# A hybrid diffusion layer in fp32 split matmuls: the order of work between the two halves, and the last stores

## The reference

```python
def rmsnorm(x, g=None):
    xf = x.astype(jnp.float32)
    y = xf * lax.rsqrt(jnp.mean(xf * xf, axis=-1, keepdims=True) + EPS)
    if g is not None:
        y = y * g.astype(jnp.float32)
    return y.astype(x.dtype)

def layer(x, cond, l, mixer):
    mod = (jax.nn.silu(cond) @ w_mod[l] + b_mod[l])[:, None, :]
    sh_m, sc_m, g_m, sh_f, sc_f, g_f = jnp.split(mod, 6, axis=-1)
    h = rmsnorm(x, norm_g[l, 0]) * (1.0 + sc_m) + sh_m
    m, ctx_out = mixer(h @ w_in[l], l)
    x = x + g_m * rmsnorm(m @ w_out[l], norm_g[l, 1])
    h = rmsnorm(x, norm_g[l, 2]) * (1.0 + sc_f) + sh_f
    a, g = jnp.split(h @ w_ffn_in[l], 2, axis=-1)
    x = x + g_f * rmsnorm((jax.nn.silu(g) * a) @ w_ffn_out[l], norm_g[l, 3])
    return x, ctx_out
```

## Time and profile before

| what | us |
|---|---|
| median of 3 timed runs (1798.84 to 1799.16) | 1798.86 |
| the profiled execution's own time | 1798.27 |
| its span, first to last instruction | 1796.4 |
| TensorE busy | 1763.2 (98%) |
| VectorE busy | 947.0 (53%) |
| ScalarE busy | 659.8 (37%) |
| GpSimd busy | 125.9 (7%) |
| FFN matmuls that take 384 columns (L1158), three passes of 1408 each | 471.4, 470.4, 470.3 |

### The profile page before, as it was taken

The page is one execution under the profiler, slowest core; times in us unless marked ns, Lnnn a source line. Parts: engine busy times, 40 slices in busy tenths (PEclk is TensorE's granted clock), DMA queues, the critical chain, the costliest instruction groups (busy, mean ns, idle before and its releaser), DMA issues.

```text
span 1796.4 us, 22651 instructions
## 1 busy us (share of the span) xinstructions
PE 1763.2 (98%) x9499; PEld 1526.4 (85%) x9499; DVE 947.0 (53%) x1276; ACT 659.8 (37%) x952; POOL 125.9 (7%) x172
## 2 busy tenths in 40 slices
PE   5999999999999999999999999999999999999998
PEld 4667666677778879999999999999999988888886
DVE  5554578633657677356656633333333455555554
ACT  3422354443464344222222222222222344454542
POOL 1001045420300010000000000000000000000000
PEclk9999999999999999999999999999999999999999
DMA  9988777775322242345454443433333333333331
GB/s 395 349 331 318 299 270 273 294 265 228 114 104 94 104 177 117 118 172 203 167 207 188 182 147 117 140 118 124 135 117 140 119 124 134 117 138 121 121 113 71
DMA packets 47046, 317.37 MB, mean 177 GB/s; under 512 B 5433, under 2 KB 7665, under 8 KB 10017
## 3 DMA queue, kind: packets, MB, share of 16 engines
q1 hardware_dynamic: 44592, 305.35, 45.4%
q0 software_dynamic: 2288, 10.56, 1.8%
q10 hardware_dynamic: 64, 0.02, 0.0%
HBM read 310.52 MB, written 5.39 MB: 176 GB/s over the span
## 4 chain that ended last, share of the span: by engine, by line
PE 93%; DVE 3%; DMA 2%; ACT 1%; issue 0%; POOL 0%; SPq 0%; DVEq 0%; POOLq 0%; ACTq 0%
PE ps L1158 41%; PE ps L934 7%; PE ps L936 7%; PE ps L935 7%; PE ps L828 7%; PE ps L829 7%; PE ps L827 7%; PE ps L806 3%; DMA raw<-in_weights 2%; PE ps L1048 1%; PE ps L1071 1%; DVE wlo L1224 1%; PE ps L1106 1%; PE ps L894 1%; PE ps L896 1%; PE ps L895 1%
## 5 line engine op out<-in xcount | busy, mean ns | idle before, releaser
L1224 DVE TENSOR_TENSOR wlo<-raw,whi 128x1024 fp32r<-128x1024 f32 x376 | 459.8, 1236 | 692.6 <-ACT whi L460 692.1
L460 ACT ACTIVATE whi<-raw 128x1024 fp32r<-128x1024 f32 x376 | 392.3, 1058 | 829.7 <-PE ps L1158 507.0
L1158 PE MATMUL ps<-h_hi,whi 128*128 128x384 f32 x1408 | 471.4, 335 | 0.5 <-DVE h_lo L1303 0.5
L1158 PE MATMUL ps<-h_hi,wlo 128*128 128x384 f32 x1408 | 470.4, 334 | 0.0
L1158 PE MATMUL ps<-h_lo,whi 128*128 128x384 f32 x1408 | 470.3, 334 | 0.0
L1158 PEld LDWEIGHTS ps<-h_hi,whi 128*128 128x128 f32 x1408 | 264.3, 188 | 0.7 <-issue 0.7
L1158 PEld LDWEIGHTS ps<-h_lo,whi 128*128 128x128 f32 x1408 | 264.3, 188 | 0.0
L1158 PEld LDWEIGHTS ps<-h_hi,wlo 128*128 128x128 f32 x1408 | 264.3, 188 | 0.0
L934 PE MATMUL ps<-whi,h_hi 128*128 128x512 f32 x624 | 259.8, 416 | 0.2 <-DVE wlo L1224 0.2
L936 PE MATMUL ps<-wlo,h_hi 128*128 128x512 f32 x624 | 244.5, 392 | 0.0
L935 PE MATMUL ps<-whi,h_lo 128*128 128x512 f32 x624 | 243.6, 390 | 0.0
(11 more groups left out here) (257 smaller groups left out, 1363.6 us busy)
## 6 DMA issues: line engine op xcount, KB each, us to landing
raw<-in_weights SPq DMA_DIRECT2D x278, 1024.0 KB, 4.9
raw_x<-in_weights SPq DMA_DIRECT2D x6, 1024.0 KB, 18.5
xT<-in_x_t SPq DMA_DIRECT2D x4, 768.0 KB, 7.0
out<-x_sb SPq DMA_DIRECT2D x6, 512.0 KB, 2.7
x_sb<-in_x_sample POOLq DMA_DIRECT2D x1, 2048.0 KB, 11.0
sbc<-silu_rows POOLq DMA_DIRECT2D x1, 2048.0 KB, 8.2
gw<-in_lru_gate_w SPq DMA_DIRECT2D x4, 256.0 KB, 3.3
out<-U POOLq DMA_DIRECT2D x4, 256.0 KB, 5.6
```

Source lines behind the costliest of these rows:

```text
L460: nc.scalar.activation(whi[:, 2 * (g % RING) + b], raw_of(t)[:, HK * b:HK * b + HK].rearrange("p k n -> p (k n)"), ACT.Copy).then_inc(w_hi, 1)
L1158: return nc.tensor.matmul(ps[bank][:, 0:T], w[:, k % KH * P:(k % KH + 1) * P], xs[:, k, :], start=first, stop=last)
L1224: V.tensor_tensor(wlo[:, 2 * SLOT[t] + b], raw_of(t)[:, HK * b:HK * b + HK].rearrange("p k n -> p (k n)"), whi[:, 2 * (g % RING) + b].bitc ...
```

## The change

Four edits. VectorE runs `residual(2)` ahead of `norm_diagonal(0)`. Block 2's squares are taken in four instructions of 512 columns (`x1_parts`), each behind its own L1609, and POOL adds four sums. In the first FFN tile pair TensorE waits for h_hi, runs the four matmuls of one k that read h_hi, then waits for h_lo and runs the two that read it. The last block is added and stored in three pieces of 1024, 512 and 512 columns (`y_parts`). The numbers of the fillers stay 26, 10 and 5.

```diff
-    xss, xrs, xsh = small("xss", 3), small("xrs", 3), small("xsh", 6)
+    xss, xrs, xsh = small("xss", 3), small("xrs", 3), small("xsh", 8)
...
+        def y_parts(tb):
+            ends = [0, D // 2, D] if tb < TB - 1 else [0, D // 2, D - NC, D]
+            return [slice(a, b) for a, b in zip(ends, ends[1:])]
+
+        def x1_parts(tb):
+            return 4 if tb == TB - 1 else 2
...
-                for b in range(2):
-                    part = slice(D // 2 * b, D // 2 * (b + 1))
+                for b, part in enumerate(y_parts(tb)):
                     sp.wait_ge(fin, 2 * tb + b + 1)
                     sp.dma_start(y_p[0, :, part] if tb == 0 else y_s[0, (tb - 1) * P:tb * P, part], x_sb[:, tb, part]).then_inc(out_st, 16)
-            sp.wait_ge(out_st, 2 * TB * 16)
+            sp.wait_ge(out_st, (2 * TB + 1) * 16)
...
-                for b in range(2):
+                w = D // x1_parts(tb)
+                for b in range(x1_parts(tb)):
                     act.wait_ge(x1_ok, 2 * tb + b + 1)
-                    nc.scalar.activation(dump[:, 2 * tb + b, :], x_sb[:, tb, D // 2 * b:D // 2 * (b + 1)], ACT.Square,
+                    nc.scalar.activation(dump[:, 2 * tb + b * w // (D // 2), b * w % (D // 2):b * w % (D // 2) + w],
+                                         x_sb[:, tb, w * b:w * (b + 1)], ACT.Square,
                                          scale=D ** -0.5, accum_out=xsh[:, 2 * tb + b:2 * tb + b + 1]).then_inc(sq_done, 1)
...
-                pe.wait_ge(x1_ok, 2 * tb + 2)
+                pe.wait_ge(x1_ok, 2 * tb + x1_parts(tb))
...
+                pe.wait_ge(h_hs, KD + k + 1)
+                for part in range(2):
+                    b, wh, wl = now[part]
+                    up(k, part, wh, h_hi, k == 0, False)
+                    up(k, part, wl, h_hi, False, False)
                 pe.wait_ge(h_ls, KD + k + 1)
                 for part in range(2):
                     b, wh, wl = now[part]
-                    ins = up_k(k, part, wh, wl)
+                    ins = up(k, part, wh, h_lo, False, k == KD - 1)
...
-                    if n % 2:
+                    if n % 2 or tb == TB - 1:
                         ins.then_inc(x1_ok, 1)
...
             residual(1)
+            residual(2)
             norm_diagonal(0)
-            residual(2)
...
-                for b in range(2):
-                    c = slice(D // 2 * b, D // 2 * (b + 1))
+                for c in y_parts(tb):
                     V.scalar_tensor_tensor(x_sb[:, tb, c], y2[:, tb, c], yrs[:, tb:tb + 1], x_sb[:, tb, c],
                                            ALU.mult, ALU.add).then_inc(fin, 1)
...
-                pool.wait_ge(sq_done, 4 + 2 * tb + 2)
-                link(G.tensor_tensor(r, r, xsh[:, 2 * tb + 1:2 * tb + 2], ALU.add))
+                for b in range(1, x1_parts(tb)):
+                    pool.wait_ge(sq_done, 4 + 2 * tb + b + 1)
+                    link(G.tensor_tensor(r, r, xsh[:, 2 * tb + b:2 * tb + b + 1], ALU.add))
```

## The result

The changed kernel takes 1802.01 us in the median of 19 runs (1800.61 to 1804.36), the kernel before 1799.16 us in 19 runs (1797.94 to 1801.35). The ratio is 1.0017 with a 95% interval of 1.001 to 1.0023: slower by about 3 us. The forecast was 1799.7 (1797.4 to 1801.5), so the direction was right and the size was not. The profiled execution has a span of 1799.8 us (1796.4 before) and took 1801.61.

A forecast was written before the change was run, and what follows sets the result against it. TensorE's pace was taken to bound the kernel behind 682 us. Terms +1.5 - 0.65 + 0 = +0.85, taken as +0.9 with the tail's +0.05, gave 1799.7 us; range 1797.4 to 1801.5, the forecast's own 1798.9 to 1800.5.

The forecast's parts named there:

- Part 1 on VectorE: Between the halves: residual 2 done 0.98 us sooner, diagonal 0 started 2.59 us later, at 675.07.
- Part 1 on TensorE, fillers in an in-order queue: Between the halves: fillers behind block 0's transposes come onto the path, block 2's transposes start 1.5 us later.
- the seams: Two passages on TensorE without a wait, allowed for in the +1.5; at 0.15 us, a released wait's cost, +1.75.
- Rival (a): Between the halves: fillers are no obstacle, diagonal 2 sets the FFN's start; -1.1 us, 1797.8; chance 0.12.
- The clock: TensorE's idle stretch before block 0's transposes: 3.75 us, where it was 1.15; the sum adds no clock loss.
- rival (c): TensorE's idle stretch before block 0 drops the clock: 0 to +6.9 us, +3.5 at half, 1803.2; chance 0.10.
- Part 2, squares in quarters: Block 2's norm: diagonal 2 0.4 us sooner, but worth nothing under TensorE's cover; quarters by themselves lose 0.3.
- Part 3, high parts lead: First FFN matmul needs only h_hi, starting 2.1 instead of 2.75 us after block 2's first transpose: -0.65 us.
- Part 4, the tail: Last block's three stores: bytes queue and end at the same time; 0, between -0.1 and +0.15 us.
- Rival (b): Last store is latency, not bytes, so a smaller one lands sooner: -0.6 us, 1799.1; chance 0.06.

The follow-up runs named there:

- e2: The changed kernel with fillers 42, 10, 5 instead of 26, 10, 5; 1800.71 us, against 1799.34 for the kernel before.
- e1: The changed kernel with fillers 42, 0, 4 instead of 26, 10, 5; 1798.71 us, against 1799.34 for the kernel before.
- e3: The changed kernel with fillers 26, 0, 0 instead of 26, 10, 5; 1800.96 us, against 1799.34 for the kernel before.
- e6: The kernel before with only residual 2 moved ahead of diagonal 0; 1802.55 us against 1799.63, ratio 1.0016.
- e12: The changed kernel with fillers 30, 10, 5 instead of 26, 10, 5; 1801.62 us, against 1799.27 for the kernel before.
- e5: The kernel before with only the high parts leading in the first FFN tile pair; 1798.70 us against 1799.63, ratio 0.9993.
- e9: The kernel before with the last block added and stored in pieces of 512, 512, 1024 columns; 1799.84 us against 1799.27.
- e8: The changed kernel with fillers 42, 0, 4, two last-block stores and squares in halves; 1797.95 us, against 1799.63 for the kernel before.
- e11: e8 with VectorE's low part of the first FFN weights moved behind diagonal 2; 1797.88 us, against 1799.27 for the kernel before.

## Why the prediction was wrong

**Part 1 on VectorE: right.** Residual 2 0.98 us sooner, diagonal 0 forecast at 675.07 against a first filler at 665.79, that is at 9.28; measured 9.27. Diagonal 2 forecast at 12.2 behind the first filler, measured 12.12.

**Part 1 on TensorE, fillers in an in-order queue: right.** +1.5 was forecast; e2 shows +1.38 where the clock stays up. The difference is the seams: three transposes behind a filler that needs no wait take 0.66 us and not 0.74. Rival (a) is out: e1 gets the -1.2 only because its fillers were moved.

**The clock: the step that failed.** The sum took the idle stretch of 3.75 us at a granted clock of 1.00 and gave rival (c) a chance of 0.10. The stretch came as forecast, 3.73 us, and the clock fell. I had read one row, the end of the kernel, where it held for 5.1 us behind the last matmul, as if it were a limit below which an idle engine is safe. The runs show that this distance is no constant: behind the last filler it was 2.1 us in the changed kernel, 2.7 in e3 and 5.1 in e6. The other bound failed too: the wait of 1.8 us near 470 us, which I called known to be harmless, is followed by a fall in five of the fourteen profiled executions (see e12). The cost was 2.46 us in the changed kernel, below the 3.5 that I had put with it, because the clock was back 5.2 us after TensorE resumed, when only block 0's transposes and nearly all of the ten fillers had run, and the transposes of block 2 ran at full rate. Over the 19 runs the excess is about 3 us (2.85 between medians), where the stretches give 1.25 without a fall and 3.71 with it: an estimate of about two executions in three with a fall, to which the 12 of 19 runs with a mean clock of 0.996 or less fit. That the share is so high is what the prediction lacked. The Trainium skill's page TensorE: Matmul & The Clock Gate, in its Part 1, says that an idle TensorE falls back to half rate. The changed kernel's trace agrees with it (0.50 within 3.73 us of idleness), while in e6 and near 472 us the fall came when TensorE was at work again. I should have given the page's rule the larger chance, since a single row stood against it.

**Part 2, squares in quarters: right.** Nothing in the changed kernel, since diagonal 2 waits 4.8 us for TensorE. Together with the new order of the residual -0.4 for the earlier diagonal was forecast, and e1 and e2 have it at 12.12 instead of 12.65, -0.53. That gain is the order's: with the order alone (e6) diagonal 2 comes at 11.86, and the quarters lose 0.26 of it, where the forecast had 0.3.

**Part 3, high parts lead: right.** -0.65 forecast, -0.64 in e5; in the changed kernel 1.99 instead of 2.75 us, with no wait behind it.

**Part 4, the tail: wrong by 0.55 us.** The argument "the bytes queue, so nothing changes" held for the first two microseconds (396 GB/s) and not for the rest: in the last 0.8 us the flow was 312, against 404 before. It takes 2.8 to 2.9 us instead of 2.6, and the last store lands 3.3 us behind its issue. I had the price of 2 KB rows at 0.15 at most. Of the 0.55 us 0.2 to 0.3 are the slower flow; where the rest goes, between the last data and the landing, stays open, and so does whether the rows of 2 KB or a small store behind others are the cause. Rival (b), a shorter last store that lands sooner, is out: it landed later.

With what the traces measured for each term the same sum reads +1.38 - 0.76 + 2.46 + 0.63 = +3.71, which is the last column of the first table.

## What to carry to other kernels

Filler matmuls are instructions in an in-order queue. When a change moves the moment for which they bridge, their number and their place have to move with it: too few before the new wait and the clock may fall, too many behind it and they are the path. Here the same change is 3 us slower with 26, 10, 5 and 1.2 us faster in the middle with 42, 0, 4.

That a granted clock survived an idle stretch once is no bound for the next one. Even the wait of 1.4 to 1.9 us near 470 us was followed by a fall in five of fourteen traces, so one trace of a kernel does not say whether a wait is harmless.

## What the hardware showed that I had not expected

- The fall of the clock can come when TensorE is at work again: in e6 1.3 us after it had resumed, and 5.1 us behind the fillers. It lasted 3.4 us in e6 and 6.8 in the changed kernel and in e3. In five of fourteen traces it also fell near 472 us, for 3.4 us, 0.6 to 1.8 us after TensorE had resumed from a wait of 1.6 to 1.8 us; other traces have a wait of up to 1.94 us there and no fall.
- While the stores of 2 KB rows ran, the flow was 352 to 377 GB/s in e9 and 312 in the last 0.8 us of the changed kernel; the kernel before, with 4 KB rows, has 404 there. Two stores of 64 partitions one behind the other move at 220.
- A POOL instruction on one column took 1.33 us beside VectorE's subtraction and 0.20 without it (e8 and e11).
- 1106 us of FFN repeat to 0.03 us over fourteen profiled executions of different kernels, while the 667 us ahead of it vary by 3 us, of which the fall near 472 us makes 1.6.
